# Two transformer layers as one straight program instead of a hardware loop

## What is computed

```python
def hybrid_layer(x, ...):
    h = rms_norm(x, g_attn_pre)
    proj = h @ w_in + b_in                       # 1024 -> 2304
    mq, mk, mv, sq, sk, sv = split(proj)         # rotary on mq, mk, sq, sk
    mo = rms_norm(moba_attention(mq, mk, mv), g_moba_out)      # 8 heads of 64
    so = rms_norm(swa_sink_attention(sq, sk, sv, sinks), g_swa_out)  # 8 q, 2 kv heads, window 128
    x = x + rms_norm(concat([mo, so]) @ w_out, g_attn_post)
    h = rms_norm(x, g_ffn_pre)
    f = silu(h @ w_gate) * (h @ w_up)            # 1024 -> 2816
    return x + rms_norm(f @ w_down, g_ffn_post)

for i in range(DEPTH):
    x = hybrid_layer(x, ..., w_in[i], ...)
```

## Time and profile before

| what | us |
|---|---|
| median of 3 runs | 617.71 |
| lowest and highest | 617.55, 620.22 |
| profiled execution: span from first to last instruction | 614.7 |
| PE busy | 588.3 |
| DVE busy | 341.2 |
| ACT busy | 286.0 |
| POOL busy | 115.8 |

### The profile page before, as it was taken

One profiled execution on the slowest core, in us unless ns is written; L12 is line 12 of the kernel. 1 busy time (PEld: TensorE's weight loads), 2 busy tenths in 40 slices (PEclk: granted clock), 3 DMA queues, 4 the chain that ended last, 5 costly groups with the idle time before them and its releaser, 6 DMA issues.

```text
span 614.7 us, 8580 instructions
## 1 busy us (share of the span) xinstructions
PE 588.3 (96%) x3028; PEld 489.9 (80%) x3028; DVE 341.2 (56%) x306; ACT 286.0 (47%) x393; POOL 115.8 (19%) x166
## 2 busy tenths in 40 slices
PE   1999999999999999999989999999999999999996
PEld 1987878888888889888877787888888888898884
DVE  3667655667545545255574756649555555442632
ACT  4474445646454344154454545546654444423520
POOL 2539520330000000000134774016000000000000
PEclk9999999999999999999999999999999999999999
DMA  9965324076665551549364823226486456333701
GB/s 307 326 201 182 113 90 166 21 256 209 235 205 181 166 201 70 206 172 319 116 209 150 297 86 136 69 103 204 141 304 205 154 190 206 138 133 142 273 1 69
DMA packets 50637, 106.83 MB, mean 174 GB/s; under 512 B 2720, under 2 KB 9120, under 8 KB 50592
## 3 DMA queue, kind: packets, MB, share of 16 engines
q1 hardware_dynamic: 50592, 106.25, 50.5%
HBM read 105.19 MB, written 1.05 MB: 173 GB/s over the span
## 4 chain that ended last, share of the span: by engine, by line
PE 86%; issue 6%; POOL 4%; DVE 2%; DMA 1%; ACT 1%; SPq 0%; POOLq 0%; DVEq 0%; ACTq 0%
PE bank L999 76%; PE bank L1013 5%; PE bank L1072 2%; PE bank L1047 2%; DMA raw<-in_w_in 1%; POOL work L426 1%; DVE w_l L707 1%; PE bank L1041 1%; ACT w_h L504 1%; POOL work L431 1%; POOL work L427 1%; POOL work L428 0%; POOL work L429 0%; DVE x L827 0%; DVE work L751 0%
## 5 line engine op out<-in xcount | busy, mean ns | idle before, releaser
L707 DVE TENSOR_TENSOR w_l<-raw,w_h 128x2048 fp32r<-128x2048 f32 x92 | 210.3, 2292 | 148.9 <-ACT w_h L504 148.9
L999 PE MATMUL bank<-w_h,actT_h 128*128 128x512 f32 (+1 forms) x624 | 241.2, 387 | 7.5 <-DVE actT_l L719 4.9
L504 ACT ACTIVATE w_h<-raw 128x2048 fp32r<-128x2048 f32 x92 | 176.0, 1915 | 139.7 <-PE bank L999 119.1
L999 PE MATMUL bank<-w_h,actT_l 128*128 128x512 f32 (+1 forms) x624 | 234.5, 376 | 0.0
L999 PE MATMUL bank<-w_l,actT_h 128*128 128x512 f32 (+1 forms) x624 | 233.7, 375 | 0.0
L999 PEld LDWEIGHTS bank<-w_h,actT_h 128*128 128x128 f32 x624 | 118.6, 190 | 30.6 <-issue 11.0
L999 PEld LDWEIGHTS bank<-w_h,actT_l 128*128 128x128 f32 x624 | 118.3, 190 | 21.5
L999 PEld LDWEIGHTS bank<-w_l,actT_h 128*128 128x128 f32 x624 | 118.8, 190 | 18.6
L445 POOL TENSOR_TENSOR norms<-norms,constants 128x1 f32<-128x1 f32 x8 | 6.7, 843 | 346.6 <-ACT work L531 346.6
L1013 PE MATMUL bank<-ident,work 128*128 128x128 f32 x332 | 48.3, 277 | 12.8 <-DVE work L731 8.0
L1013 PEld LDWEIGHTS bank<-ident,work 128*128 128x128 f32 x332 | 40.3, 142 | 20.4 <-issue 10.8
(11 more groups left out here) (65 smaller groups left out, 371.1 us busy)
## 6 DMA issues: line engine op xcount, KB each, us to landing
raw<-in_w_gate SPq DMA_DIRECT2D x22, 1024.0 KB, 5.0
raw<-in_w_up SPq DMA_DIRECT2D x22, 1024.0 KB, 5.0
raw<-in_w_down SPq DMA_DIRECT2D x22, 1024.0 KB, 4.8
raw<-in_w_in SPq DMA_DIRECT2D x18, 1024.0 KB, 7.0
raw<-in_w_out SPq DMA_DIRECT2D x8, 1024.0 KB, 5.1
bias<-in_b_in SPq DMA_DIRECT2D x8, 256.0 KB, 5.7
x<-in_x SPq DMA_DIRECT2D x2, 512.0 KB, 6.7
gain_a<-in_g_attn_pre SPq DMA_DIRECT2D x2, 512.0 KB, 5.7
```

Source lines behind the costliest of these rows:

```text
L504: nc.scalar.activation(w["h"][:, slot(b), :], raw[:, r, :], ACT.Copy).then_inc(hi_ready, 1)
L707: nc.vector.tensor_tensor(w["l"][:, slot(b), :], raw[:, slot(b, RAW), :], w["h"][:, slot(b), :].bitcast(F32), ALU.subtract).then_inc(lo_re ...
L999: ins = nc.tensor.matmul(bank[BANK_OF[name]][:, 0:n], left[s][:, at + k, tokens(t)], right[r][:, k, c * BANK:c * BANK + n], start=first an ...
```

## The change

On all five engines the hardware loop becomes a Python `for`, so that both layers are written out one behind the other, and `L` is a constant when the program is built. Each `If` becomes a Python `if`, so its body stands in the program once, for layer 0. All waits get constant targets, and all addresses are constants. The counter `n_step` of `link` now runs on over both layers, so the target of its wait is the counter itself.

```diff
-            with sp.Fori(0, depth) as L:
+            for L in range(depth):
                 for b in range(RAW + 1, NB):
                     load_block(L, b)
...
-                with sp.If(L < depth - 1):
-                    following = nc.s_assert_within(
-                        L + 1, 1, depth - 1, skip_runtime_bounds_check_because="L < depth - 1 here")
+                if L < depth - 1:
+                    following = L + 1
...
-                pool.wait_ge(pool_step, L * PER_LAYER + n_step[0])
+                pool.wait_ge(pool_step, n_step[0])
...
-            with pool.Fori(0, depth) as L:
+            for L in range(depth):
...
-                with pool.If(L < depth - 1):
+                if L < depth - 1:
                     rms_x(L + 1, 0, 0)
                 rms_y(L, 1, 1)
-                with pool.If(L < depth - 1):
+                if L < depth - 1:
                     rms_x(L + 1, 0, 1)
...
-            with act.Fori(0, depth) as L:
+            for L in range(depth):
...
-                with act.If(L < depth - 1):
+                if L < depth - 1:
...
-                dve.wait_ge(dve_step, L * PER_LAYER + n_step[0])
+                dve.wait_ge(dve_step, n_step[0])
...
-            with dve.Fori(0, depth) as L:
+            for L in range(depth):
...
-                with dve.If(L < depth - 1):
+                if L < depth - 1:
                     dve.wait_ge(x_ready, X_READY.done(L, (1, 0)))
                     scale_rows(L + 1, 0, 0)
...
-            with pe.Fori(0, depth) as L:
+            for L in range(depth):
                 rows_landed(L, 0, 0)
...
-                        with pe.If(L < depth - 1):
+                        if L < depth - 1:
                             rows(L + 1, 0, 0)
```

More of the change, by code:

```diff
@@ L481, in _ @@
                 rms_y(L, 1, 0)
-                with pool.If(L < depth - 1):
+                if L < depth - 1:
                     rms_x(L + 1, 0, 0)
                 rms_y(L, 1, 1)
-                with pool.If(L < depth - 1):
+                if L < depth - 1:
                     rms_x(L + 1, 0, 1)
-                assert n_step[0] == PER_LAYER, n_step
+                assert n_step[0] == (L + 1) * PER_LAYER, n_step
         @block.scalar
```

## The result

| | before | changed |
|---|---|---|
| median of 10 runs each, us | 620.20 | 614.00 |
| lowest and highest, us | 616.37, 621.22 | 612.38, 616.23 |
| profiled execution: span, us | 614.7 | 610.8 |
| profiled execution: its own time, us | not recorded | 612.58 |

The changed kernel is faster, by less than one per cent: 0.9927 of the time before, with a 95% interval of 0.9906 to 0.9948, which is 3.2 to 5.8 us. The medians are 6.2 us apart where 3.8 were predicted, because the ten executions of the kernel before have a median of 620.20 us and not the 617.71 from which the prediction started. The 614.0 us next to the predicted 613.9 is luck: five of the ten executions lie between 612.38 and 613.05 us and five between 614.95 and 616.23, and the median falls into the gap between them.

A forecast was written before the change was run, and what follows sets the result against it. PE was taken as the bound, busy 588.3 of 614.7 us. Gains of 3.36 us at the layer boundary and 0.46 us of register arithmetic, 3.82 us together, taken from 617.71 gave 613.9 us; range 612.4 to 615.4.

The forecast's parts named there:

- the base: Around the profiled span: the 3.0 us between it and the median of 617.71 us stays.
- the rival of a gain spread over the run: Both layers: shorter queues of all engines spread the gain, the seam shrinking by less than 2 us; no chance given.
- Items 1 and 2: Layer boundary: without the jumps back, PE's next matmul starts 2.70 us earlier and DVE's projection 3.37 us earlier.
- One sign: On ACT at the layer boundary: the table load would stand right behind the sum of squares.
- Items 3 and 4: POOL's rotary step at the boundary: starts 3.36 us earlier, its first operation still 2.30 us; transposes come at 321.03.
- Rival A: Boundary: POOL's first rotary operation gets ahead of DVE's split; 4.5 us gained, 613.2 us; chance 0.10.
- Item 5: Before the boundary's transposes: PE waits 0.70 us; gain 3.36 us; PE's saving alone nothing, DVE's alone at most 1.36.
- Item 7: Hand-overs between engines: removed register arithmetic saves 0.46 us, bounds 0 and about 1.0.
- Item 9: Whole run: straight-line instruction page fetches of the longer program, as many per layer as before, cost nothing.
- rivals C and D: C: DVE still stops near the boundary, 617.3 or 615.6 us, chance 0.07; D: late PE page fetches, 619.3 us, 0.04.
- Rival B: Boundary: PE's gap is a data wait, the branch merely overlaps; only register arithmetic saved, 617.3 us; chance 0.06.

The follow-up runs named there:

- the hint: Kernel before with all loops, register arithmetic and branches kept, each loop arming a prefetch of its jump's target: ratio 0.9942 (0.9913 to 0.9972).
- the reordered kernel with its loops: Kernel before, loops kept, with only a DVE weight split moved behind POOL's rotary step in both layers: median 615.43 us, ratio 0.9959.
- the reordered kernel: Changed kernel with a DVE weight split moved behind a projection and POOL's rotary step in both layers: medians 609.91 and 609.78 us in two runs.
- POOL's long loop: Changed kernel, but POOL keeps its loop, with 256 more instructions in its body: one execution of 612.58 us, seam 10.75 us.

## Why the prediction was right, and where it was not

- **The step that failed: the base, and with it the clock.** The prediction took the 3.0 us between the span of one profile and the median of three executions for something round the span that stays, and put at nothing what differs between executions of one kernel. In all thirteen profiles whose time is known 1.8 us lie round the span. The other 1.2 us, and the 2.5 us by which the ten later executions of before have a still higher median (620.20), are more of what the prediction left out, and the granted clock goes with it: of 69 later executions of before 19 have a mean granted clock of 0.998 or more, with a median of 616.48 us, and 50 have less, with 619.2. Of the 26 of the changed kernel 13 have 0.998 or more, with 612.82, and 13 have 0.991 to 0.995, with 614.99. So at a high clock the change is worth 3.7 us, and the 6.2 us between the medians of the first ten of each are this and a difference in how often the clock was low. The clocks of the first ten of before are not on record, so the share of each can't be told.
- **Where the gain is**: at the seam, as said. 13.77 us before, 10.26 after, in all three profiles of the changed kernel; 3.51 us against the 3.36 worked out. The rest of layer 1 moved along unchanged (283.85 and 283.70), and so did layer 0 from the 121st matmul to its last (274.99 and 275.07), so the rival of a gain spread over the run is out.
- **Items 1 and 2** (PE restarts 0.23 us behind its last matmul, DVE projects right behind `scale_rows`): both as described. One sign failed, at no cost: ACT has no table load at the seam any more, it stands at 334.41 ahead of the first exponentials (L552). Only with the hint, where the loops stay, is it right behind the sum of squares, at 315.7.
- **Items 3 and 4** (POOL begins right behind its norm step and still loses two microseconds to DVE's split): POOL's start at 316.83, measured from PE's last matmul of layer 0, is 3.33 us earlier than before (3.36 expected), and its first operation takes 2.12 us instead of 2.30. These 0.18 us more make up the difference at the seam (3.33 + 0.18 = 3.51). Rival A, POOL ahead of DVE, did not come about.
- **Item 5** (PE waits 0.70 us; PE's part alone is worth nothing, DVE's alone up to 1.36): 0.65, 0 and 1.67. DVE's part is larger than said because I took the idle time of the row for the delay: matmul records overlap, so 1.36 us idle is 1.52 us later from start to start, and PE's gap at its own jump happened to be 2.79 us from start to start instead of 2.94. The order of the two stops was right.
- **Item 7**, register arithmetic at 0.46 us: wrong, it is next to nothing. I had taken every part of a gap that held a register instruction for its cost. The largest piece, 0.22 us at the start, was not there: PE's first weight matmul begins at 14.80 us in the changed kernel's first profile and at 14.55 in its second, and at 14.65 with the hint, which keeps all registers, where it was 14.86. The hand-over at 50 did get shorter (PE's gap from start to start 1.58 us before, 1.59 with the hint, 1.39 after), but with new waits elsewhere, such as 0.5 us for ACT at 71, nothing of it is left in layer 0.
- **Item 9 and rivals C and D** (page fetches in straight code): no wait of this kind in the changed kernel's profile. Its page has 24 instruction transfers on q8, PE's queue, where there were 26.
- **Rival B** (the gap is a wait for data): refuted by PE written out alone, with DVE's program as before, and by the prefetch.
- **The span.** The profiled execution of before took some 616.5 us (an estimate: 614.7 + 1.8) and not the median 617.71. Like for like the gain is 614.7 - 610.8 = 3.9 us. Of these 3.51 are the seam, and 0.4 is the clock of TensorE, which rose at 18.2 us instead of 19.1 at the start (the 121st matmul begins at 35.19 and at 35.63 us). That is chance and not the change: in the reordered kernel with its loops it rose at 18.2 too, and the same matmul begins at 35.17.

So the mechanism was right and the seam was met to 0.15 us. The span was met because a register term of 0.46 us too much was made up for by 0.15 too little at the seam and a chance 0.4 from the clock. The time was met by luck, and the difference of the medians was missed, since the prediction looked at one profile, in which the clock was steady.

How often the clock falls in a kernel isn't settled, nor whether the change itself makes falls rarer. It fell in nine of the fourteen profiles, each time during a wait of PE of 1.1 to 4.2 us or within a microsecond behind it. But three profiles with such waits have no fall (before, the first of the changed kernel, and POOL's long loop), so the wait doesn't decide it. The two profiles of the reordered kernel, whose longest wait behind the start is 0.65 us, have none. None of its ten executions has a mean granted clock below 0.997, where half of the 26 executions of the changed kernel have 0.995 or less, and none of the ten is more than 1.8 us above their lowest, while 11 of the 26 are 2.5 us or more above theirs. Since five of the last six of these 26 had a high clock with the wait still there, this is strong support for the reading and no proof.

## What to carry to other kernels

A loop back over a long body stopped the queues of four engines for 2.6 to 6.2 us, once each (bodies of 127 and 247 traced instructions went on in 0.2 to 0.3); look for it as "issue" on the idle side of an engine and as a long COMPARE_BRANCH in a queue, since the wait's label can name an innocent tile. The instruction queues among the DMAs show it too. Price it on the chain, not per engine: stops on several engines cover each other, so that half the cure (PE alone) was worth nothing. Writing out the loop or prefetching its target removes it alike, and in the changed kernel the order of one DVE split against one POOL step was worth 2.8 us more. And before a change of a few microseconds is priced in the median of a few executions, see how far executions of one kernel lie apart: here 4 to 5 us, with the granted clock.

## What the hardware showed that was not expected

A wait of the matrix engine can cost more than its length. With a wait of 4.16 us the granted clock was 0.50 for 6.8 us and the work behind it took 2.0 us longer, so that removing one of two stops, which merged two waits into a long one, brought no gain (1.0021, interval 0.9999 to 1.0043). Behind waits of 1.1 to 1.3 us the fall lasted 3.4 us and cost 1.5 us, in some executions and not in others. And a DVE split of two fp32 operands in SBUF held back a POOL operation that began during it: 2.1 to 2.7 us instead of 0.3 to 0.7. At the seam of the changed kernel the split is over at 318.76 and the held operation at 318.95, and when the split was moved, the long operation moved with it.
